# Hybrid decoder trunk: the table from expert slots to tokens built from rank rows and expert rows

## The reference

```python
_, gsel = lax.top_k(glog, 1)
elog_g = jnp.take_along_axis(elog, gsel[:, :, None], axis=1)[:, 0]
top_v, top_i = lax.top_k(elog_g, EXPERT_TOP_K)
...
for e in range(N_EXPERTS):
    y = (jax.nn.silu(t @ w_gate[e]) * (t @ w_up[e])) @ w_down[e]
    out = out + combine[:, e:e + 1] * y
```

## Time and profile before

| | us |
|---|---|
| median of 3 runs | 1165.65 |
| the runs | 1164.91 to 1169.02 |
| profiled execution | 1171.51 |
| its span, first to last instruction | 1169.8 |
| PE busy | 1117.0 |
| DVE busy | 891.3 |
| ACT busy | 647.8 |

### The profile page before, as it was taken

The page is one execution under the profiler, slowest core; times in us unless marked ns, Lnnn a source line. Parts: engine busy times, 40 slices in busy tenths (PEclk is TensorE's granted clock), DMA queues, the critical chain, the costliest instruction groups (busy, mean ns, idle before and its releaser), DMA issues.

```text
span 1169.8 us, 15565 instructions
## 1 busy us (share of the span) xinstructions
PE 1117.0 (95%) x5528; PEld 834.1 (71%) x5528; DVE 891.3 (76%) x1133; ACT 647.8 (55%) x809; POOL 123.2 (11%) x160
## 2 busy tenths in 40 slices
PE   7999999799999999999999899999999999999994
PEld 5777777477776777777775888878867777777772
DVE  5254556867689999999999462454689999999997
ACT  5123444511257888888884321232357888888872
POOL 3000000112122000000004100000121000000022
PEclk9999999989999999999999899999989999999998
DMA  8642222220259999999998433233159999999984
GB/s 310 191 135 73 81 81 73 83 79 1 72 173 363 385 405 392 402 404 399 408 410 288 159 110 106 72 108 108 73 188 370 395 398 405 397 398 410 406 315 165
DMA packets 77605, 286.43 MB, mean 245 GB/s; under 512 B 16648, under 2 KB 16648, under 8 KB 61165
## 3 DMA queue, kind: packets, MB, share of 16 engines
q1 hardware_dynamic: 65212, 241.64, 54.3%
q0 software_dynamic: 8608, 30.95, 8.1%
q10 hardware_dynamic: 3728, 13.11, 2.8%
HBM read 266.79 MB, written 20.20 MB: 245 GB/s over the span
## 4 chain that ended last, share of the span: by engine, by line
PE 83%; DVE 12%; issue 2%; ACT 1%; POOL 1%; DMA 1%; DVEq 0%; POOLq 0%; SPq 0%; ACTq 0%; PEldq 0%
PE ps L1689 25%; PE ps L1691 24%; PE ps L1690 24%; DVE w_split L966 3%; DVE x_sb L1395 2%; PE ps L2028 1%; DVE arena L1332 1%; DVE arena L987 1%; PE ps L1941 1%; PE ps L1896 1%; PE ps L1777 1%; DVE arena L1160 1%; PE ps L1962 1%; PE ps L1664 1%; PE ps L2052 1%
## 5 line engine op out<-in xcount | busy, mean ns | idle before, releaser
L966 DVE TENSOR_TENSOR w_split<-ring,w_split 128x1024 fp32r<-128x1024 f32 x452 | 540.0, 1220 | 80.1 <-ACT w_split L622 68.6
L622 ACT CAST w_split<-ring 128x1024 fp32r<-128x1024 f32 x452 | 470.9, 1051 | 184.6 <-PE ps L1691 181.4
L1689 PE MATMUL ps<-w_split,hT 128*96 128x512 f32 (+2 forms) x976 | 387.5, 397 | 8.4 <-DVE hT L1451 4.0
L1691 PE MATMUL ps<-w_split,hT 128*96 128x512 f32 (+2 forms) x976 | 380.3, 390 | 0.0
L1690 PE MATMUL ps<-w_split,hT 128*96 128x512 f32 (+2 forms) x976 | 380.2, 390 | 0.0
L1689 PEld LDWEIGHTS ps<-w_split,hT 128*96 128x96 f32 (+1 forms) x976 | 163.9, 168 | 72.1 <-issue 8.5
L1691 PEld LDWEIGHTS ps<-w_split,hT 128*96 128x96 f32 (+1 forms) x976 | 163.6, 168 | 60.2
L1690 PEld LDWEIGHTS ps<-w_split,hT 128*96 128x96 f32 (+1 forms) x976 | 164.1, 168 | 54.1
L1689 PE MATMUL ps<-hT,w_split 128*128 128x512 f32 (+1 forms) x384 | 146.1, 381 | 2.1 <-PE ps L1691 1.5
L1690 PE MATMUL ps<-hT,w_split 128*128 128x512 f32 (+1 forms) x384 | 143.7, 374 | 0.0
L1691 PE MATMUL ps<-hT,w_split 128*128 128x512 f32 (+1 forms) x384 | 143.6, 374 | 0.0
(11 more groups left out here) (246 smaller groups left out, 889.8 us busy)
## 6 DMA issues: line engine op xcount, KB each, us to landing
ring<-in_exp_w_gate SPq DMA_DIRECT2D x64, 1024.0 KB, 10.5
ring<-in_exp_w_up SPq DMA_DIRECT2D x64, 1024.0 KB, 10.4
ring<-in_exp_w_down SPq DMA_DIRECT2D x64, 1024.0 KB, 10.9
ring<-in_w_in_even SPq DMA_DIRECT2D x14, 1024.0 KB, 11.1
y_rows_dram<-arena ACTq DMA_DIRECT2D x32, 384.0 KB, 7.0
ring<-in_w_in_odd SPq DMA_DIRECT2D x12, 1024.0 KB, 6.8
ring<-in_w_out_even SPq DMA_DIRECT2D x4, 1024.0 KB, 4.9
h_rows_dram<-arena POOLq DMA_DIRECT2D x8, 512.0 KB, 4.1
```

The costliest lines, as they stand in the source:

```text
L622: s.copy(hi_of(c), raw(c)).then_inc(hi_ready, 1)
L966: v.tensor_tensor(lo_of(c), raw(c), hi_of(c).bitcast(F32), ALU.subtract).then_inc(lo_ready, 1)
L1689: mm(out, a[0], b[0], start=start, stop=False)
L1691: return mm(out, a[0], b[1], start=False, stop=stop)
```

## The change

The 0/1 matrix per expert goes. For each pick k (first and second), each token has one expert and one slot, so the table is a sum of eight products (pick k, tile t): a matrix `slot_hot[k, t]` (token by slot, from the token's rank row) times `tok_pick[k, t]` (token by expert, the token's number in the picked expert's column), 96x16 out, all added up in one PSUM region. `slot_picks` makes both operands at the end of the routing; `slot_index(l)` and `slot_tokens(l)` run once per layer. Expert 15's own matrix `sel_last` is made by one instruction in step 0. The subtraction that yields the second pick moves from `result_rows` to `slot_picks`.

```diff
--- before.py
+++ after.py
@@ -161,7 +161,9 @@
         y_back = part(0, TT, 2, D)
-        sel = arena[:, 4096:8192].bitcast(F16).rearrange("p (t e c) -> p t e c", t=TT, e=E)
+        slot_hot = arena[:, 4096:4480].bitcast(F16).rearrange("p (k t c) -> p k t c", k=2, t=TT)
+        tok_pick = arena[:, 4480:4544].bitcast(F16).rearrange("p (k t n) -> p k t n", k=2, t=TT)
+        sel_last = arena[:, 4544:4736].bitcast(F16).rearrange("p (t c) -> p t c", t=TT)
         sel_first = part(8192, TT, CAP)
@@ -403,7 +405,7 @@
         PARTS = tuple((t, half) for t in (2, 3, 0, 1) for half in range(2))
-        IDX_BANK = (2, 7, 7, 7)
+        IDX_BANK = 2
         LOGIT_BANK = (4, 4, 4, 7)
@@ -566,8 +568,8 @@
                 for e in range(1, E):
-                    if e == 1 or e % 4 == 0:
-                        pool.wait_ge(idx_ready, 4 * l + e // 4 + 1)
+                    if e == 1:
+                        pool.wait_ge(idx_ready, l + 1)
                     if e >= 2:
@@ -1327,15 +1329,19 @@
-            def select(g, tiles):
-                for t in tiles:
-                    ins = v.tensor_tensor(sel[:, t, 4 * g:4 * g + 4, 0:CAP], bc(place[:, t, 4 * g:4 * g + 4], 2, P, 4, CAP),
-                                          bc(slot_iota[:, 0:CAP], 1, P, 4, CAP), ALU.is_equal)
-                return ins
-            def slot_tokens(l, g):
-                dve.wait_ge(idx_full, 4 * l + g + 1)
-                v.tensor_copy(slot_tok[0:CAP, 4 * g:4 * g + 4], ps[0:CAP, IDX_BANK[g], 4 * g:4 * g + 4]).then_inc(idx_ready, 1)
+            def slot_picks(l):
+                link(v.tensor_tensor(picks[:, 1, :, :], member, picks[:, 0, :, :], ALU.subtract))
+                link(v.tensor_tensor(picked, bc(place, 1, P, 2, TT, E), picks, ALU.mult))
+                link(v.tensor_reduce(row_rank, picked, AX, ALU.add))
+                v.tensor_tensor(tok_pick, picks, tok_id[:, :].unsqueeze(1).unsqueeze(3).broadcast_to([P, 2, TT, E]), ALU.mult)
+                v.tensor_tensor(slot_hot.rearrange("p k t c -> p (k t) c"),
+                                bc(row_rank.rearrange("p k t -> p (k t)"), 2, P, 2 * TT, CAP),
+                                bc(slot_iota[:, 0:CAP], 1, P, 2 * TT, CAP), ALU.is_equal).then_inc(sel_ready, 1)
+            def slot_tokens(l):
+                dve.wait_ge(idx_full, l + 1)
+                v.tensor_copy(slot_tok[0:CAP, :], ps[0:CAP, IDX_BANK, 0:E]).then_inc(idx_ready, 1)
@@ -1365,15 +1371,13 @@
                 place_pair(l)
-                for g in range(2):
-                    select(g, (0, 1))
                 scaled(n, 3)
                 place_tile(l, 3)
-                select(0, (2, 3)).then_inc(sel_ready, 1)
+                slot_picks(l)
                 v.tensor_tensor(g_exp, lg[:, :, 0:GROUPS], bc(top_g, 2, P, TT, GROUPS), ALU.subtract).then_inc(route_arg, 1)
@@ -1401,7 +1405,6 @@
-                link(v.tensor_tensor(picks[:, 1, :, :], member, picks[:, 0, :, :], ALU.subtract))
                 rank = rank_sb[:, 0:TT * E].rearrange("p (t n) -> p t n", t=TT)
@@ -1497,15 +1500,11 @@
                 copy_first_xgT(l)
-                slot_tokens(l, 0)
+                slot_tokens(l)
                 splits(c0 + 4)
                 keep_ranks(l)
-                splits(c0 + 6)
-                select(1, (2, 3)).then_inc(sel_ready, 1)
-                splits(c0 + 8)
-                select(2, range(TT)).then_inc(sel_ready, 1)
-                splits(c0 + 9)
-                select(3, range(TT)).then_inc(sel_ready, 1)
+                v.tensor_tensor(sel_last, bc(place[:, :, E - 1], 2, P, TT, CAP), bc(slot_iota[:, 0:CAP], 1, P, TT, CAP),
+                                ALU.is_equal).then_inc(sel_ready, 1)
                 splits(c0 + 10)
@@ -1526,8 +1525,6 @@
                 step(1, n0 + 1, 1, step_chunk(l, 1), None, None, with_y=False)
-                for g in range(1, 4):
-                    slot_tokens(l, g)
                 for e in (2, 3, 4):
@@ -2010,15 +2007,15 @@
                 gather_first(3)
-                slot_index(l, 0)
-            def slot_index(l, g):
-                pe.wait_ge(sel_ready, 4 * l + g + 1)
-                for e in range(4 * g, 4 * g + 4):
+                slot_index(l)
+            def slot_index(l):
+                pe.wait_ge(sel_ready, 2 * l + 1)
+                for k in range(2):
                     for t in range(TT):
-                        last = mm(ps[0:CAP, IDX_BANK[g], e:e + 1], sel[:, t, e, 0:CAP], tok_id[:, t:t + 1],
-                                  start=(t == 0), stop=(t == TT - 1))
+                        last = mm(ps[0:CAP, IDX_BANK, 0:E], slot_hot[:, k, t, :], tok_pick[:, k, t, :],
+                                  start=(k == 0 and t == 0), stop=(k == 1 and t == TT - 1))
                 last.then_inc(idx_full, 1)
@@ -2083,9 +2080,9 @@
                 down(n - 1, 0, c, None, bank=5)
-                pe.wait_ge(idx_ready, 4 * l + 4)
+                pe.wait_ge(sel_ready, 2 * l + 2)
                 for t in range(TT):
-                    last = mm(ps[0:CAP, 7, t * P:(t + 1) * P], sel[:, t, E - 1, 0:CAP], ident16[:, :], start=True, stop=True)
+                    last = mm(ps[0:CAP, 7, t * P:(t + 1) * P], sel_last[:, t, :], ident16[:, :], start=True, stop=True)
                 last.then_inc(last_sel_turned, 1)
@@ -2131,21 +2128,17 @@
-                def step(n, u, c, i, landed_next, first=False, indices=False, midway=None):
+                def step(n, u, c, i, landed_next, first=False, midway=None):
                     gate_or_up(1, u, c + 4, i)
-                    if indices:
-                        for g in range(1, 4):
-                            slot_index(l, g)
                     turn_xg(n + 1, 1 - u, landed_next)
                     n = n0 + e
-                    step(n, e % 2, step_chunk(l, e), None, landed(l, e + 1), first=(l == 0 and e == 1),
-                         indices=(e == 1))
+                    step(n, e % 2, step_chunk(l, e), None, landed(l, e + 1), first=(l == 0 and e == 1))
                 with pe.Fori(0, E // 2 - 3) as i:
```

## The result

| | before | after |
|---|---|---|
| median, us (11 runs each) | 1165.34 | 1158.62 |
| lowest to highest | 1162.18 to 1169.02 | 1154.42 to 1162.06 |
| ratio, 95% interval | | 0.9938 [0.9924, 0.9953] |
| profiled execution | 1171.51 | 1158.24 |
| its span and mean granted clock | 1169.8, 0.979 | 1156.2, 0.984 |

The two profiled executions lie 13.3 us apart, twice the difference of the medians.

What follows compares the result with a forecast made beforehand. PE, busy 1117 of 1170 us, was taken as the bound, with a wait for DVE at gate(1). Gains of 4.28 (products) and 4.32 (selections) sum to 8.6 us: median 1165.65 becomes 1157.05, range 1154 to 1162.5 for 8 in 10.

Steps and rivals of the forecast that it cites:

- The 48 products: Expert 1: one-column products leave PE's queue, where nothing hid them; gain 2.14 us per layer, 4.28 for two.
- The ten selections: Expert 0, DVE: one remains, the copy of expert 1's tokens comes earlier, gate(1)'s wait goes whole; 2.22 and 2.10, sum 4.32.
- sits ahead of a copy: Layer 0, 339 to 353 us: DVE work feeding only a table stands before the copy of expert 1's tokens, which PE awaits.
- From then on DVE is ahead by as much as PE is: After gate(1)'s wait goes, the splits of expert 1 and 2 stay ahead of their use; no size given.
- The table made at once: End of routing, DVE: five instructions take 2.04 us in place of 1.02; idle time before expert 0's copies takes up 1.02.
- PE at the same place: Start of expert 0: first product waits 0.15 us for the first copy, off the 0.32 gather wait; landing unmoved, cost 0.
- The four selections ahead of `scaled`: Routing, tile 3: they go, `scaled` starts up to 1.9 us earlier, but PE's logits hold the next start; gain taken as 0.
- The sum: Whole kernel: 4.28 + 4.32 = 8.6 us, so the median 1165.65 becomes 1157.05.
- A: Rival, expert phase: weight loads take the gain back, the products' 4.3 us (1161.4) or all of it (1165.6); chance 0.10.
- B: Rival, gate(1): expert 1's copy stays late if its gather lands 2.9 us later; only the products gain, 1161.4; chance 0.08.
- C: Rival, end of routing: the table's five linked instructions take 1.0 us longer per layer; gain 6.6, 1159.05; chance 0.10.
- D: Rival, routing into expert 0: PE's lower clock level lasts longer; at 10 us more, 10 us lost, 1167.1; chance 0.04.

Runs made afterwards that it cites:

- selections late: Kernel after with nine spare 128x384 comparisons per layer on DVE, all behind the copy of expert 1's tokens: 1161.06 us, ratio 0.9961 to before.
- both back: Kernel after with nine spare comparisons in expert 0 and 48 spare one-column products in expert 1, at their old places: 1167.50 us, ratio 1.0016 to before.
- Selections back: Kernel after with nine spare 128x384 comparisons per layer at their old places on DVE in expert 0: 1162.54 us, ratio 0.9962 to before.

## Why the prediction was right

- *The 48 products*, 4.28: right in place and size. They left PE's queue, and putting them back costs 2.14 us per layer.
- *The ten selections*, 4.32: right in size, 8.74 less 4.28 being 4.46. Gate(1) follows the last up product without a wait in both layers, and DVE's copy now waits for ACT, as forecast. What "sits ahead of a copy" suggests was too narrow, though: the place ahead of the copy is not what costs (selections late). What counts is that the selections take about 2.2 us more per layer than DVE has to spare, in this stage and the next.
- *"From then on DVE is ahead by as much as PE is"*: right; the steps from expert 2 on are 17.57 us.
- *The table made at once*: forecast 2.04 us with a compare of 0.95; measured 2.06 and 0.95. It used up DVE's idle time, and the cast came 1.08 us behind the first table product on PE (336.44 less 335.36; 1.18 in the earlier trace rows).
- *PE at the same place, "cost 0", "the landing doesn't move"*: the step that was not right. Expert 0's first product does wait for the first copy, as forecast (the copy ends at 335.92, the product starts at 335.98), but it came no 0.15 later: it starts 2.57 us behind the start of `gather_first`'s last products in layer 0 and 2.35 in layer 1, where it was 2.54 in both. The gather landed later instead: cast to transposes 9.04 us in layer 0 where it was 8.35, and PE waited 0.96 in place of 0.32. That gave back 0.59 us in layer 0 and nothing in layer 1. The cast was not late, so it is the transfer. From the cast to the transposes it was 8.18 to 8.87 us in the eight layers traced with the old table and 8.11 to 9.05 in the fourteen with the new one and the cast at the same place; the wait lay between none and 1.16 us, and both back had 0.30 in layer 0 and 1.16 in layer 1 of one execution. So it is scatter of a transfer among the weight loads, and a price of the change doesn't show in it. What the change does is to expose it: the wait at gate(1) had hidden this scatter.
- *The four selections ahead of `scaled`*, 0: right. DVE was done sooner and then waited 0.83 us for the logits, as the rows show (start, us, idle before, releaser):

```profile
323.63 0.18 DVE L1257 TENSOR_TENSOR arena<-ps,b_route 128x20 f32<-128x20 f32 x1 [0.83 <-PE ps L1938]
```

- *The sum*: 8.6 forecast; 8.74 less 0.43 in the traces' stages (0.59 back in layer 0, 0.16 gained in layer 1), 7.95 +- 0.44 and 8.25 +- 0.62 at equal clock. The medians show 6.72 (1165.34 less 1158.62), 1.9 less than the sum, so the time came out 1.5 above the forecast of 1157.1. I subtracted the sum from a median of three runs and took the clock to be alike; it moves single runs of a kernel by 4 us to either side. At equal clock 0.4 to 0.7 of the 1.9 is left (8.6 less 8.25 and 7.95). That the rest is clock is inferred: the clocks of these eleven runs of before are not on record.

Of the rivals, A did not happen. ACT's waits from 336 to 637 us still name PE for the weight pieces and no load:

```profile
ACT w_split L624 <- PE ps L1688: 43.9, 140, 0.6
```

and layer 0's experts moved as many bytes per second as before:

```profile
336.00:600.00 264.00, 262.91 (x1255) 188.07 (x1256) 251.50 (x253) 217.82 (x243) 15.38 (x16) 1.00 1.01 394
```

The Trainium skill (DMA: Bandwidth & Descriptors, Where 436 GB/s comes from) puts the HBM side at about 358 GB/s per core, half of a stack's 716. This phase runs above that figure before and after, and the products' saving did not return as a wait for weights. B's condition, a gather 2.9 us late, was not met: the largest wait for it was 1.16 us in any run, and DVE's copy still ended in time. B was misread in one point: its 0.7 us are no reserve against a late gather, because PE itself waits for the gather at the transposes, and there all of its lateness counts (24.98 and 24.36 us above, with waits of 0.96 and 0.47). C did not happen: the five instructions kept to their rows. The sign that I had named for it, a longer wait at expert 1's transposes, was there, but the landing made it, not the table. D did not either: the stretches at the lower clock end with the routing in the kernel after, and the window above has 1.00 from 336 us on. Even a wait of 1.67 us at gate(1) leaves it there. Selections back, behind its wait:

```profile
351.20:363.00 11.80, 11.80 (x57) 8.44 (x58) 11.80 (x12) 8.38 (x11) 0.00 (x0) 1.00 0.98 340
```

## What to carry to other kernels

When an engine off the bound holds up the bound once, ask how much it has to do up to the next point where it is waited for, not only what stands directly ahead of the wait: moving 4.4 us of work behind the first wait here only moved the wait. A wait can also hide another one: with the wait for DVE gone, PE pays for every late gather. Work that the bounding engine runs itself, however small its instructions, counts in full (48 products of one column, 2.14 us). And compare stages, from one instruction of the bound to another, before spans: two profiled executions of the same change lay 13.6 us apart, of which some 5 had nothing to do with it.

## What the runs showed of the hardware

- 0.001 of mean granted clock went with 0.75 us of time over 156 runs of all kernels. The runs of the kernel before spread over 0.978 to 0.988, which at that rate is 7.5 of the 9.2 us by which their times spread (1162.37 to 1171.57). Part of it comes whole: from the first gate products of layer 0's mixer to the filler products at its end PE took 230.9 to 231.2 us in five of the thirteen profiles (both of before, one of two of after among them), whose granted clock fell at 250 to 260 us, and 228.4 to 229.9 in the others.
- Behind eight f16 products with 16 moving columns and 96 stationary ones PE went on after 0.62 us in layer 0 and 0.50 in layer 1. In both it was DVE's copy that it waited for (in layer 0 the copy ends at 335.92, 0.06 us before PE's product), so the products take 62 ns each at most; 16 of one column took 0.70, 44 ns each. Sixteen times the columns cost less than one and a half times the time.
